# Two expert products before the row weights, and the last expert pair's result combined by one-hot matmuls

## What is computed

```python
def hier_moe(hn, w_group, w_expert, w_gate, w_up, w_down):
    ...   # eid, w: top-1 of 4 groups, top-2 of its 8 experts, and their weights per token
    comb = jnp.sum(jax.nn.one_hot(eid, N_EXPERTS, dtype=jnp.float32) * w[..., None], axis=1)
    out = jnp.zeros(t.shape, jnp.float32)
    for e in range(N_EXPERTS):                       # 32 experts, FF = 256
        a = jax.nn.silu(t @ w_gate[e]) * (t @ w_up[e])
        out = out + comb[:, e:e + 1] * (a @ w_down[e]).astype(jnp.float32)
    return out.astype(hn.dtype).reshape(b, l, d)
...
    x = x + jnp.concatenate([o_r, o_s], axis=-1) @ w_out      # retention and attention heads
    x = x + hier_moe(rmsnorm(x, norm2_g), ...)
```

## Time and profile before

| | us |
|---|---|
| median of three runs | 617.01 (613.02 to 618.59) |
| the profiled execution, its time | 616.9 |
| its span | 615.1 |
| TensorE busy in the span | 505.9 |
| VectorE, ScalarE, GpSimd busy | 239.0, 144.0, 152.9 |
| mean granted TensorE clock | 0.915 of full |

### The profile page before, as it was taken

The page is one execution under the profiler, slowest core; times in us unless marked ns, Lnnn a source line. Parts: engine busy times, 40 slices in busy tenths (PEclk is TensorE's granted clock), DMA queues, the critical chain, the costliest instruction groups (busy, mean ns, idle before and its releaser), DMA issues.

```text
span 615.1 us, 7687 instructions
## 1 busy us (share of the span) xinstructions
PE 505.9 (82%) x2854; PEld 315.1 (51%) x2854; DVE 239.0 (39%) x558; ACT 144.0 (23%) x361; POOL 152.9 (25%) x289
## 2 busy tenths in 40 slices
PE   3596988999999999899993489999888777797820
PEld 3585766776777676487782433343333333332300
DVE  2856768768431465722126321221111111101017
ACT  4543363535535213122010010110000000001000
POOL 5074745112304645523011211111111111001010
PEclk9898999799999999989996589999888998979775
DMA  8430030022025003166629539999999999999449
GB/s 255 185 95 19 8 135 2 2 69 69 2 70 201 23 1 104 51 274 267 263 76 404 229 148 417 423 423 424 423 424 427 424 425 425 425 425 422 185 161 343
DMA packets 33446, 140.68 MB, mean 229 GB/s; under 512 B 5760, under 2 KB 8912, under 8 KB 21120
## 3 DMA queue, kind: packets, MB, share of 16 engines
q1 hardware_dynamic: 25568, 126.87, 51.6%
q0 software_dynamic: 4816, 9.67, 4.3%
q10 hardware_dynamic: 3024, 3.64, 1.8%
HBM read 133.44 MB, written 13.63 MB: 239 GB/s over the span
## 4 chain that ended last, share of the span: by engine, by line
PE 44%; SPq 20%; DVE 12%; DMA 8%; issue 4%; ACT 4%; POOL 2%; ACTq 0%; DVEq 0%; POOLq 0%
PE banks L900 19%; SPq L624 14%; PE banks L1122 9%; SPq L632 6%; DMA w_moe_a<-in_w_up_dram 4%; PE banks L1137 3%; PE banks L958 2%; DMA w_moe_a<-y_d 2%; POOL w_lo L756 1%; PE banks L1116 1%; PE banks L1075 1%; PE banks L1043 1%; PE banks L1038 1%; DMA rows<-hn_d,idx 1%; PE banks L992 1%
## 5 line engine op out<-in xcount | busy, mean ns | idle before, releaser
L756 POOL TENSOR_TENSOR w_lo<-w_raw,w_hi 128x512 fp32r<-128x512 f32 x52 | 69.1, 1345 | 126.4 <-ACT w_hi L1288 124.6
L1122 PE MATMUL banks<-w_moe_a,xgT 128*64 128x512 f32 x272 | 89.0, 669 | 10.8 <-DMA w_moe_a<-in_w_up_dram 10.8
L1122 PE MATMUL banks<-w_moe_b,xgT 128*64 128x512 f32 x240 | 78.1, 644 | 18.7 <-DMA w_moe_a<-in_w_up_dram 10.8
L1857 DVE SCALAR_TENSOR_TENSOR glu<-banks,wr,glu 128x256 f32<-128x256 f32 x16 | 7.7, 484 | 146.8 <-ACT glu L1414 146.8
L802 POOL DMA_INDIRECT y_d<-y_sb,idx x16 | 16.0, 999 | 195.3 <-PE banks L1116 131.3
L900 PE MATMUL banks<-w_hi,xT_hi_a 128*128 128x512 f32 (+4 forms) x140 | 58.0, 414 | 7.0 <-ACT sv L1256 7.0
L1122 PEld LDWEIGHTS banks<-w_moe_b,xgT 128*64 128x64 f32 x240 | 24.8, 147 | 63.0 <-issue 60.8
L900 PE MATMUL banks<-w_lo,xT_hi_a 128*128 128x512 f32 (+4 forms) x140 | 55.3, 395 | 0.0
L900 PE MATMUL banks<-w_hi,xT_lo_a 128*128 128x512 f32 (+4 forms) x140 | 54.9, 392 | 0.0
L1122 PEld LDWEIGHTS banks<-w_moe_a,xgT 128*64 128x64 f32 x272 | 27.6, 154 | 40.3 <-issue 40.0
L1414 ACT ACTIVATE glu<-banks,wr 128x256 f32<-128x256 f32 x16 | 7.6, 474 | 153.5 <-PE banks L1122 153.5
(11 more groups left out here) (248 smaller groups left out, 816.7 us busy)
## 6 DMA issues: line engine op xcount, KB each, us to landing
w_moe_a<-in_w_down_dram SPq DMA_DIRECT2D x22, 1024.0 KB, 25.8
w_moe_a<-in_w_gate_dram SPq DMA_DIRECT2D x17, 1024.0 KB, 21.1
w_moe_a<-in_w_up_dram SPq DMA_DIRECT2D x17, 1024.0 KB, 24.6
w_moe_b<-in_w_gate_dram SPq DMA_DIRECT2D x15, 1024.0 KB, 24.5
w_moe_b<-in_w_up_dram SPq DMA_DIRECT2D x15, 1024.0 KB, 25.5
w_moe_b<-in_w_down_dram SPq DMA_DIRECT2D x10, 1024.0 KB, 26.7
w_raw<-in_w_in_dram SPq DMA_DIRECT2D x36, 256.0 KB, 4.5
x_sb<-in_x_prompt_dram SPq DMA_DIRECT2D x8, 512.0 KB, 7.1
```

The costliest lines, as they stand in the source:

```text
L756: nc.gpsimd.tensor_tensor(w_lo[:, s, :], w_raw[:, s, :], w_hi[:, s, :].bitcast(F32), ALU.subtract).then_inc(split, 1)
L1122: l = mm(acc[64 * e:64 * e + 64, u, :].rearrange("p (m f) -> p m f", m=2), xgT[:, xu, k, 64 * e:64 * e + 64], units(at_e[e], 2)[:, :, k * ...
```

## The change

- The order of the beginning. TensorE transposes pair 0's rows and then pair 1's, these into PSUM banks 2 and 3, and makes gate and up of pair 0 and of pair 1 in a row. The 20 small products for `wr` come behind. VectorE scales pair 0's rows ahead of the softmax steps. ScalarE does a sigmoid of one column ahead, which loads its table. SyncE waits for both gathers before it issues down of pair 1 and what follows.
- `y_d` is filled with zeros by nine DMAs from a table of zeros in DRAM, issued by SyncE during attention; GpSimd's first scatter waits for them.
- The order of the last weights is gate and up of 14, down of 13, down of 14, gate and up of 15, down of 15. Gate and up of 15 come in 16 DMAs of 256 KiB, four for each quarter of the sum over D, down of 15 in 4 of 512 KiB, two for each half of the output columns, and TensorE waits by quarter and by half.
- The last pair isn't scattered. ScalarE copies its result to `y_last[:, 0]` (fp32r), VectorE puts the rest of the rounding into `y_last[:, 1]`, and TensorE multiplies both by a one-hot of token by row (`oh_last`, built by VectorE from `idx`) into PSUM, one tile of tokens after the other. `y_d` is read back as soon as pair 14's scatter has landed, into units 10 to 14. GpSimd adds the two choices of tiles 1 to 4 (`y_two`); VectorE adds that sum, and then PSUM, to `x_sb`; tile 0's two choices are both added by VectorE.

The core of the diff:

```diff
 NUNIT = UNITS_A + UNITS_B
+FIN_UNIT, YTOK_UNIT = 6, 10
+LAST = NPAIR - 1
+YOUT = [16 * (NPAIR // 2), 16 * (NPAIR // 2 - 1)]
+FIN_BANKS = [0, 4, 6, 2, 0]
 CAP = 64
...
         def gu_unit(p, e):
-            return (0 if p == 0 else 6 * p - 2) + 2 * e
+            return (0 if p == 0 else 6 * p - 2 if p < LAST else 6 * p) + 2 * e
         def dn_unit(p, e):
-            return (6 * p + 8 if p < NPAIR - 1 else 6 * p + 4) + e
+            return (6 * p + 8 if p < LAST - 1 else 6 * p + 4) + e
         def units(i, n):
...
                 load_weights(OUT0, k)
+            for i in range(2 * T_TOK // P):
+                sp.dma_start(y_d[P * i:P * i + P, :], consts[:, NCONST:NCONST + D]).then_inc(y_zero, 16)
             sp.wait_ge(o_lo, len(UNITS))
...
             load_gu(2)
+            for u in range(2):
+                sp.wait_ge(xg_in[u], 16)
             load_dn(1)
-            for p in range(3, NPAIR):
+            for p in range(3, LAST):
                 for e in range(2):
...
                 gather(p)
-            for p in range(NPAIR):
+            pool.wait_ge(y_zero, 16 * (2 * T_TOK // P))
+            for p in range(LAST):
                 if p + 4 < NPAIR:
...
                         pool.sem_inc(L_done, 1)
+            for t in range(1, NT):
+                R = out_rows(t)
+                pool.wait_ge(yg_in[t], 32)
+                nc.gpsimd.tensor_tensor(y_tok(t, 0)[0:R, :], y_tok(t, 0)[0:R, :], y_tok(t, 1)[0:R, :], ALU.add
+                                        ).then_inc(y_two, 1)
...
             find_rows(0, pair_dst, row_oh, oh_ready).then_inc(idx_ps, 1)
-            def rows_T(u):
+            def rows_T(u, into=side):
                 gv = xg[:, u, :].rearrange("p (q k) -> p k q", k=KD)
                 for k in range(KD):
-                    l = nc.tensor.transpose(side[:, k // 4, (k % 4) * P:(k % 4) * P + P], gv[:, k, :], ident)
+                    l = nc.tensor.transpose(into[:, k // 4, (k % 4) * P:(k % 4) * P + P], gv[:, k, :], ident)
                 return l
...
                 act_T().then_inc(aT_ps, 1)
+            def gate_up_last():
+                u = LAST % 2
+                pe.wait_ge(xg_ev, LAST + 1)
+                for k in range(KD):
+                    if k % 2 == 0:
+                        pe.wait_ge(gu_last[k // 2], raw_all + 64)
+                    for e in range(2):
+                        l = mm(acc[64 * e:64 * e + 64, u, :].rearrange("p (m f) -> p m f", m=2),
+                               xgT[:, u, k, 64 * e:64 * e + 64], units(gu_unit(LAST, e), 2)[:, :, k * FF:k * FF + FF],
+                               start=(k == 0), stop=(k == KD - 1))
+                l.then_inc(gu_ps, 1)
+            def down_last():
+                pe.wait_ge(aT_ev, LAST + 1)
+                pe.wait_ge(y_ev, LAST)
+                for n in range(2):
+                    pe.wait_ge(dn_last[n], raw_all + 32)
+                    for j in range(2):
+                        for e in range(2):
+                            l = mm(acc[64 * e:64 * e + 64, 2 + n, :], actT[:, j, 64 * e:64 * e + 64],
+                                   units(dn_unit(LAST, e), 1)[:, 0, j * D + n * 512:j * D + n * 512 + 512],
+                                   start=(j == 0), stop=(j == 1))
+                    l.then_inc(y_ps, 1)
+            def last_rows(i, t, n):
+                R, b = out_rows(t), FIN_BANKS[i] + n
+                pe.wait_ge(yl_hi, n + 1)
+                pe.wait_ge(yl_lo, n + 1)
+                cols = slice(n * 512, n * 512 + 512)
+                mm(banks[0:R, b, :], oh_last[:, t, 0:R], y_last[:, 0, cols], start=True, stop=False)
+                return mm(banks[0:R, b, :], oh_last[:, t, 0:R], y_last[:, 1, cols], start=False, stop=True)
             def down_of(p):
...
             rows_of_pair(0)
+            pe.wait_ge(xg_in[1], 16)
+            rows_T(1, acc[:, 2:4, :]).then_inc(xg_ps, 1)
+            gate_up_of(0)
+            gate_up_of(1)
             pe.wait_ge(wr_ready, 1)
             find_rows(32, pair_wr, row_oh.bitcast(F32)).then_inc(wr_ps, 1)
-            rows_of_pair(1)
-            gate_up_of(0)
-            for p in range(1, NPAIR):
-                if p + 1 < NPAIR:
-                    rows_of_pair(p + 1)
+            rows_of_pair(2)
+            act_T_of(0)
+            down_of(0)
+            for p in range(2, LAST):
+                rows_of_pair(p + 1)
                 act_T_of(p - 1)
                 down_of(p - 1)
-            act_T_of(NPAIR - 1)
-            down_of(NPAIR - 1)
+            act_T_of(LAST - 1)
+            down_of(LAST - 1)
+            gate_up_last()
+            act_T_of(LAST)
+            down_last()
...
                         down((4, 5)).then_inc(L_y, 1)
+                pe.wait_ge(L_ye, NPAIR * (LEVELS - 1) + 1)
+            pe.wait_ge(oh_fin, 1)
+            pe.wait_ge(aT_ev, NPAIR)
+            for n in range(2):
+                for i in range(3):
+                    l = last_rows(i, i, n)
+                    if n:
+                        l.then_inc(fin_ps, 1)
+            for i in (3, 4):
+                if i == 4:
+                    pe.wait_ge(y_fin, 1)
+                for n in range(2):
+                    l = last_rows(i, i, n)
+                l.then_inc(fin_ps, 1)
...
             af(small[:, 20:25], small[:, 25:30], ACT.Exp).then_inc(r_expd, 1)
+            af(small[:, 155:156], ident[:, 0:1], ACT.Sigmoid)
             def pair_out(p):
...
             pair_exp(0)
-            for p in range(1, NPAIR):
+            for p in range(1, LAST):
                 pair_exp(p)
                 pair_out(p - 1)
-            pair_out(NPAIR - 1)
+            pair_out(LAST - 1)
+            pair_exp(LAST)
+            for n in range(2):
+                act.wait_ge(y_ps, NPAIR + n)
+                nc.scalar.copy(y_last[:, 0, n * 512:n * 512 + 512], acc[:, 2 + n, :]).then_inc(yl_hi, 1)
...
             step(nc.vector.memset(level0[:, :], 0.0))
+            rows_in(0)
             dve.wait_ge(r_expd, 1)
...
                                       ).then_inc(aT_ev, 1)
-            rows_in(0)
+            rows_in(1, acc[:, 2:4, :])
             dve.wait_ge(wr_ps, 1)
             dve.sem_inc(wr_ev, 1)
-            rows_in(1)
             for p in range(NPAIR):
                 actT_in(p)
+                if p == LAST - 1:
+                    step(nc.vector.tensor_copy(small[:, 156:157], idx[:, LAST:NPAIR]))
+                    for t in range(NT):
+                        l = stt(out=oh_last[:, t, :], in0=iota, scalar=float(P * t - 1),
+                                in1=small[:, 156:157].to_broadcast([P, P]), op0=ALU.add, op1=ALU.is_equal)
+                    l.then_inc(oh_fin, 1)
+            for n in range(2):
+                dve.wait_ge(yl_hi, n + 1)
+                tt(y_last[:, 1, n * 512:n * 512 + 512], acc[:, 2 + n, :],
+                   y_last[:, 0, n * 512:n * 512 + 512].bitcast(F32), ALU.subtract).then_inc(yl_lo, 1)
...
                                               ).then_inc(L_ae, 1)
-            for t in range(NT):
-                R = out_rows(t)
+            for i in range(NT):
+                t, R = i, out_rows(i)
                 dve.wait_ge(yg_in[t], 32)
-                for k in range(2):
+                if t:
+                    dve.wait_ge(y_two, t)
+                for k in range(1 if t else 2):
                     step(tt(x_sb[0:R, t, :], x_sb[0:R, t, :], y_tok(t, k)[0:R, :], ALU.add))
-                dve.sem_inc(y_fin, 1)
+                dve.wait_ge(fin_ps, i + 1)
+                b = FIN_BANKS[i]
+                tt(x_sb[0:R, t, :], x_sb[0:R, t, :], banks[0:R, b:b + 2, :].rearrange("p b n -> p (b n)"), ALU.add
+                   ).then_inc(y_fin, 1)
```

65 lines of the change are left out of this document (47 added, 18 removed).

## The result

| | before | after |
|---|---|---|
| median of four runs each, us | 617.09 (613.02 to 618.59) | 609.53 (607.63 to 611.8) |
| ratio, 95% interval | | 0.9875 [0.9831, 0.9919] |
| the profiled execution, its time | 616.9 | 611.8 |
| its span | 615.1 | 610.0 |

The change makes the kernel 1.25% faster. The forecast was 605.9 us with a range of 600 to 612; the time lies 3.6 us above the forecast and inside the range.

A forecast was written before the change was run, and what follows sets the result against it. The expert stage was taken as bound by loading weights, plus the first product's start and what follows the stream. Span 615.1 - 6.0 (front) - 12.5 (tail) + 7.5 (final adds) = 604.1, plus 1.8: 605.9 us, range 600 to 612.

The forecast's parts named there:

- the front: Experts' beginning: pair 0's gate and up product ends at 356.8 instead of 362.8, -6.0 us; bounds -2.4 and -9.5.
- the early reading of y: Stream's end: y read once pair 14's scatter lands, 575.2 instead of 593.71; -18.5 us in all, 12.5 from the tail.
- the turns: Final adds: VectorE instructions with two SBUF inputs and GpSimd's SBUF-reading adds exclude each other; +7.5 us with, +2.8 without.
- the final adds: Behind y's reads: VectorE and GpSimd adds end at +25.45 us instead of +18.0, costing +7.5 us.
- the slices: Last pair's weights in small DMAs: about 398 GB/s instead of 424, costing 0.9 us.
- each us earlier there is a us off the whole stream: Experts' beginning: an earlier end of the first gate and up product shortens the weight stream equally, -6.0 us taken.
- The zeros: Zero fill of y_d by nine DMAs during attention: costs nothing; 11 to 22 us without that cover.
- rival 3: Last six weight units slowed to between 398 and 227 GB/s: up to 12.0 us more, 617.9 at most; chance 0.10.
- Rival 1: Final adds: GpSimd and VectorE don't hinder each other, 4.7 us less, 601.2 us; chance 0.14.
- rival 4: Final adds: GpSimd's four chained adds decide from 5.4 us each, over 1% slower from 6.9; chance 0.04.
- Rival 2: Experts' beginning: clock stays at 1.2 GHz through the first product, -2.4 instead of -6.0, 609.5 us; chance 0.14.
- Rival 5: Scatter lands in 3 to 6 us and the clock rises earlier: 599 to 602 us; chance 0.06.

The follow-up runs named there:

- the run without the wait: Changed kernel without SyncE's wait for the two gathers ahead of down of pair 1, TensorE's order kept: 610.17 us, 0.9857.
- the tail alone: Changed kernel with the old order of the beginning (TensorE, VectorE, SyncE's hold, early sigmoid undone), all else kept: 614.43 us, 0.9938.
- whole units: Changed kernel with the last pair's weights in six whole DMAs of 1 MiB again: 611.5 us, 0.9893.
- tile 0's y ahead: Changed kernel with VectorE adding tile 0's two y before its subtractions for the last pair: 608.2 us, 0.9822.
- y one tile ahead: Changed kernel with one fp32 one-hot product, no subtractions, all adds on VectorE, next tile's y added before each PSUM add: 606.41 us, 0.9815.
- the fp32 one-hot: Changed kernel with one fp32 one-hot matmul instead of two fp32r, no subtractions, all y adds on VectorE: 608.13 us, 0.9845.

## Why the prediction was right, and where it was off

The forecast of 605.9 us had the mechanisms of the front, of the early reading of y and of the turns right; one step failed, the final adds, the slices were undersized, and the front's number came out near in part by luck.

**The front, -6.0 us: near in the result, by luck in part.** Two errors stood against each other, and a third took some of it back. The gathers landed 5.3 us after their start (342.60 to 347.91), the first one 4.5, not 3.3. The clock was full at 350 (0.58 from 345 to 350, 1.00 in the next stretch), some 4 us after TensorE's start and not 10.7; so the product took half of 13.88. From the row list pair 0's product ends 8.0 us earlier, between the -6.0 taken and the bound of -9.5. But "each us earlier there is a us off the whole stream" did not hold: 5.4 of the 8.0 us reach pair 14 (217.5 to 212.1). The stream did stay fed, as forecast: in the trace the DMA engines are full in every stretch from 350 to 400. But the four held units were to land near 354 and were still being moved at 356.71, so the units that the product frees stood behind them. In the run without the wait the product came 5.5 us earlier and pair 14's 5.3: there each us did count. And at the end less is left: the last add comes 3.0 to 4.1 us earlier than in the tail alone, and the ratios differ by 0.6%, about 4 us.

**The zeros at nothing: right,** by the 150.2 and 150.3 us above.

**The reading of y, -18.5 us: right.** It starts 19.1 us earlier from the list (255.6 to 236.4). The scatter landed in 7.1 us, taken at 8.4.

**The slices, 0.9 us: undersized.** They cost 3.0 us in after against whole units (2.7 to 3.5 in the profiles in which TensorE waits for the last one; in two others at most 2.0 and 1.7), at 291 to 352 GB/s between 555 and 570. The forecast's sign for this, near 400 GB/s over the last 15 us of weights, failed with it. That is rival 3 in its mechanism, well short of its 12. Down of pair 15, issued up to 567.3, then had its last piece 14.1 us later, at 581.4. The shorter product behind the last slice pays for it, so it did not show in the total.

**The final adds, +7.5 us: the step that failed.** "So the weights' arithmetic is hidden under the reading of y, by a thin margin at the first tile" is wrong, and so is "VectorE tile 0's y adds 4.8 to 7.3". The first product by the one-hot was to be ready near 582, behind "half of down at the low clock 1.7". In the trace the last quarter of gate and up lands at 576.30, and behind it stand the quarter's product 1.94, the sigmoid 0.48, two products by VectorE 0.97, transposes and a copy of 0.96 and all of down, 5.35: down's weights were there when it came to them, its input was late. The prediction began this path at the last slice of down. By its own sum the last quarter of gate and up lands two units, 4.9 us, ahead of that 576.5, which is 233.4 from the list; it landed at 236.2, and what stood behind it was not in the sum. And 1.7 is half of down at the full clock (3.63 for all of it in the earlier trace rows); at the low clock the first half took about 3.3 us, until ScalarE began its copy at 584.25. VectorE does its work in order, and the two subtractions stand ahead of all adds, so the first y add is at 588.07, 11.55 us behind the first read instead of 4.8. The last add is at +30.07, predicted +25.45, before +17.97: the term is +12.1 and not +7.5. These 4.6 us late, less 0.6 for the earlier read, are the 4.0 by which the span from the row list missed, and the medians missed by 3.6. Three runs agree: tile 0's y ahead starts at +4.8 and ends at +25.7, y one tile ahead ends at +25.9, the fp32 one-hot starts at +7.6 and then waits for TensorE. With y one tile ahead the last add, at 262.2 from the list, is where the prediction had it for the changed kernel (262.5). That the later tiles landed late as well, tile 3 at +17.3 where GpSimd was to start on it at +14.0, did not set the end: from 588.07 on VectorE has no gap.

**The turns: right.** GpSimd's adds took 2.39 and 2.43 us (taken as 2.6), and VectorE's beside them 5.21 for two instead of 2.48, 2.84 and 2.12 instead of 1.22: 5.3 us in all. Rival 1, no hindrance, is out, and rival 4 too, since no add of GpSimd's came near 5.4. The Trainium skill (SBUF — State Buffer, Who interferes with whom) has a VectorE instruction contend with a GpSimd one that reads SBUF when it has two inputs in SBUF, and not when it has at most one. The trace agrees: the adds of PSUM into x took 1.22 beside GpSimd's, as at 593.31 and 593.85. What the prediction did not draw from this is that the division of the adds was then worth nothing, as the run with VectorE alone shows. Rival 2 had the clock wrong: it was full. Rival 5's earlier clock came true, and its landing nearly (7.1 against at most 6), but not its time, for the reason above.

Open stays how much of after's 5.35 us for down of pair 15 is chance: in seven of the experiments it took 3.65, at a clock that was still full, in the other four 5.2 to 5.4, among them the changed kernel run once more. Open too is what sets that clock, and why the front's 5.4 us in the stream are only 3.0 to 4.1 at the last add.

## What to carry to other kernels

When work is moved under a wait, ask of each engine that does it in which order it stands there: an instruction that comes late holds up those behind it whose data are there, and the gain of an early read is lost again. A second engine that takes turns with the first can cost it what it takes off, here 5.3 us of turns for four adds of 1.24, so time the work with one engine before dividing it. Holding transfers back for a short one is worth nothing if what is gained then waits behind the held bytes.
